# Attention weights times values in one encoder layer on one Trainium2 core: one fp32 product, or three fp32r products with low parts made on VectorE

## What is computed

```
logits = einsum('bqhcd,bkhcd->bhcqk', q, k) * scale + bias        # c = 0, 1; 512 x 512
p      = softmax(logits)
attn   = p[:, :, 0] - lam * p[:, :, 1]
out    = einsum('bhqk,bkhe->bqhe', attn, v)                       # v: 512 keys x 128
out    = rmsnorm(out, subln_g) * (1 - lambda_init)
```

## Time and profile before

| | |
|---|---|
| median of 3 runs | 968.12 us (967.98 to 968.15) |
| the profiled execution | 968.37 us, of which the span of instructions is 966.5 us |
| PE busy | 959.1 us, 99% of the span |
| DVE busy | 690.2 us, 71% |
| ACT busy | 439.5 us, 45% |
| granted TensorE clock, mean | 0.999 of full speed |

### The profile page before, as it was taken

One profiled execution on the slowest core, in us unless ns is written; L12 is line 12 of the kernel. 1 busy time (PEld: TensorE's weight loads), 2 busy tenths in 40 slices (PEclk: granted clock), 3 DMA queues, 4 the chain that ended last, 5 costly groups with the idle time before them and its releaser, 6 DMA issues.

```text
span 966.5 us, 15092 instructions
## 1 busy us (share of the span) xinstructions
PE 959.1 (99%) x5483; PEld 826.3 (85%) x5483; DVE 690.2 (71%) x1067; ACT 439.5 (45%) x699; POOL 87.9 (9%) x104
## 2 busy tenths in 40 slices
PE   9999999999999999999999999999999999999998
PEld 8889999999888887677777878889999999988887
DVE  6888897787754438868898755789897788743333
ACT  6445665546333233234454563446565554622222
POOL 0011121210011010000000000001112121000100
PEclk9999999999999999999999999999999999999999
DMA  6356767675433336121221332256777767333322
GB/s 231 139 142 170 194 166 193 179 184 150 137 97 101 98 124 241 66 83 51 83 85 44 121 109 91 95 142 154 191 189 171 197 169 190 100 104 98 90 68 87
DMA packets 55029, 128.67 MB, mean 133 GB/s; under 512 B 5954, under 2 KB 14287, under 8 KB 54724
## 3 DMA queue, kind: packets, MB, share of 16 engines
q1 hardware_dynamic: 44452, 107.31, 34.4%
q0 software_dynamic: 10384, 20.67, 12.3%
q10 hardware_dynamic: 144, 0.05, 0.1%
HBM read 123.78 MB, written 4.22 MB: 132 GB/s over the span
## 4 chain that ended last, share of the span: by engine, by line
PE 91%; DVE 5%; issue 2%; ACT 2%; DMA 0%; DVEq 0%; SPq 0%; ACTq 0%
PE bank L2159 14%; PE bank L2161 14%; PE bank L2160 14%; PE bank L2215 8%; PE bank L2216 8%; PE bank L2217 8%; PE bank L2207 6%; PE bank L2209 3%; PE bank L2656 1%; PE bank L2657 1%; PE bank L2658 1%; PE bank L2548 1%; DVE xt_both L1383 1%; PE bank L2302 1%; PE bank L2303 1%
## 5 line engine op out<-in xcount | busy, mean ns | idle before, releaser
L1220 DVE TENSOR_TENSOR w_lo<-raw,w_hi 128x1024 fp32r<-128x1024 f32 (+1 forms) x94 | 113.2, 1205 | 110.2 <-ACT w_hi L634 109.9
L634 ACT CAST w_hi<-raw 128x1024 fp32r<-128x1024 f32 (+1 forms) x94 | 95.0, 1011 | 187.5 <-PE bank L2161 172.5
L2159 PE MATMUL bank<-x_hi,w_hi 128*128 128x512 f32 x320 | 128.5, 402 | 0.1
L2160 PE MATMUL bank<-h_lo,w_hi 128*128 128x512 f32 x330 | 128.4, 389 | 0.0
L2161 PE MATMUL bank<-x_hi,w_lo 128*128 128x512 f32 x320 | 124.8, 390 | 0.0
L2160 PE MATMUL bank<-x_lo,w_hi 128*128 128x512 f32 x320 | 124.6, 389 | 0.0
L2215 PE MATMUL bank<-xt_both,w_hi 128*128 128x256 f32 x408 | 115.6, 283 | 1.0 <-ACT chain L786 1.0
L2217 PE MATMUL bank<-xt_both,w_lo 128*128 128x256 f32 x408 | 115.5, 283 | 0.0
L2216 PE MATMUL bank<-xt_both,w_hi 128*128 128x256 f32 x408 | 115.5, 283 | 0.0
L2215 PEld LDWEIGHTS bank<-xt_both,w_hi 128*128 128x128 f32 x408 | 78.2, 192 | 1.4 <-issue 1.4
L2217 PEld LDWEIGHTS bank<-xt_both,w_lo 128*128 128x128 f32 x408 | 78.2, 192 | 0.0
(11 more groups left out here) (382 smaller groups left out, 2138.0 us busy)
## 6 DMA issues: line engine op xcount, KB each, us to landing
raw<-in_ffn_w_down SPq DMA_DIRECT2D x32, 512.0 KB, 3.6
raw<-in_ffn_w_gate SPq DMA_DIRECT2D x25, 512.0 KB, 3.9
raw<-in_ffn_w_up SPq DMA_DIRECT2D x25, 512.0 KB, 4.4
raw<-in_w_in SPq DMA_DIRECT2D x24, 512.0 KB, 3.3
raw<-in_ffn_w_gate SPq DMA_DIRECT2D x34, 256.0 KB, 3.1
raw<-in_ffn_w_up SPq DMA_DIRECT2D x34, 256.0 KB, 3.1
raw<-in_ffn_w_down SPq DMA_DIRECT2D x16, 384.0 KB, 3.1
sums<-in_ffn_w_gate SPq DMA_DIRECT2D x17, 256.0 KB, 3.6
```

The source lines that it names most:

```text
L634: nc.scalar.copy(w_hi[:, half, 0:kb, :], raw[:, slot, 0:kb, :]).then_inc(w_hi_made, 1)
L1220: nc.vector.tensor_tensor(w_lo[:, half, 0:kb, :], raw[:, slot, 0:kb, :], w_hi[:, half, 0:kb, :].bitcast(F32), ALU.subtract).then_inc(w_spl ...
L2159: nc.tensor.matmul(dst, w_hi[:, half, k, :], hi, start=first and k == 0, stop=False)
L2160: nc.tensor.matmul(dst, w_hi[:, half, k, :], lo, start=False, stop=False)
```

## The change

It does five things.

1. The product of weights and values becomes three fp32r matmuls: v_hi by attn_hi, v_lo by attn_hi, v_hi by attn_lo. ACT's copies become casts to fp32r, as many as before. DVE gets five subtractions more for each head: `v_low(h)` and `attn_low(h, 0 to 3)`, 20 in all, each 128 x 512, reading a bank and the high part.
2. PE waits for these: the third matmul of a key block for its low part, a turn for the low part that frees its bank.
3. `attend_turns` moves ahead in the k-tile: behind group 5 of tile 13, behind group 4 of tiles 17 and 21. ACT takes the turned blocks ahead of the casts of q and k, and the cast of the next but one weight tile (15, 19, 23) behind them.
4. On DVE the low parts stand ahead of spectral pairs and of w_lo for tiles 14, 18 and 22, and some pairs move behind them, past the head's end.
5. Two small things far from there: the load of the lambdas counts on another semaphore, and one wait of DVE on itself uses a common counter.

```diff
-        v_nat, _ = place("v_nat", [P, NT, P], at=act3_at)
+        v_hi, _ = place("v_hi", [P, NT, P], F32R, at=act3_at)
+        v_lows = [place(f"v_lo{n}", [P, NT, P], F32R, at=at)[0] for n, at in enumerate((vx_at + 4 * S, bias_at))]
+        attn_hi, _ = place("attn_hi", [P, NT, S], F32R, at=attn_t_at)
```

ACT, the end of head 1 (heads 0 and 2 are alike):

```diff
             split(8, N_MIX + 18)
+            attn_turns(1, (0, 1))
             qk_high(2, 0)
-            attn_turns(1, (0, 1))
-            split(8, N_MIX + 19)
             qk_high(2, 1)
             attn_turns(1, (2, 3))
+            split(8, N_MIX + 19)
             attended(1)
```

DVE, the new functions:

```diff
+            def v_low(h):
+                dve.wait_ge(v_set, h + 1)
+                nc.vector.tensor_tensor(v_low_part(h)[:], bank[TURN_BANKS[h]][:].rearrange("p (t c) -> p t c", t=NT),
+                                        v_hi[:].bitcast(F32), ALU.subtract).then_inc(v_split, 1)
+
+            def attn_low(h, kt):
+
+                dve.wait_ge(attn_turned, NT * h + kt + 1)
+                dve.wait_ge(attn_t_set, NT * h + kt + 1)
+                nc.vector.tensor_tensor(attn_low_part(h, kt)[:], bank[4 + kt % 2][:], attn_hi[:, kt, :].bitcast(F32),
+                                        ALU.subtract).then_inc(attn_split, 1)
```

DVE, the end of head 0:

```diff
             combine(0, 3)
-            cross_far(0)
-            split(8, N_MIX + 14)
+            v_low(0)
+            attn_low(0, 0)
+            attn_low(0, 1)
             project(13)
             split_qk(1, 0)
+            attn_low(0, 2)
             split_qk(1, 1)
+            attn_low(0, 3)
+            split(8, N_MIX + 14)
+            cross_far(0)
             own_near(0)
             split(8, N_MIX + 15)
```

DVE, the end of head 1 and the begin of head 2 (at the end of head 2 `real_parities(1)` and `imaginary_parities(1)` move behind the low parts and w_lo of tile 22 in the same way):

```diff
             att_means(0)
-            imaginary_parities(0)
+            v_low(1)
             project(16)
-            split(8, N_MIX + 18)
-            cross_near(1)
+            attn_low(1, 0)
+            attn_low(1, 1)
             project(17)
             split_qk(2, 0)
+            attn_low(1, 2)
             split_qk(2, 1)
+            attn_low(1, 3)
+            split(8, N_MIX + 18)
+            imaginary_parities(0)
+            cross_near(1)
+            split(8, N_MIX + 19)
+
+            logits(2, 0)
             cross_far(1)
-            split(8, N_MIX + 19)
-
-            logits(2, 0)
-            own_near(1)
             combine(2, 0)
             logits(2, 1)
-            own_far(1)
+            own_near(1)
             project(18)
             combine(2, 1)
+            own_far(1)
             imaginary(1)
```

PE (`turn`, `attend`, and tile 17 for three tiles), and the two small things of point 5:

```diff
             def turn(h, kt):
-                wait(pe, attn_t_set, NT * h + kt - 1)
+                wait(pe, attn_split, NT * h + kt - 1)
...
                 for kt in range(NT):
                     pe.wait_ge(attn_t_set, NT * h + kt + 1)
-                    ins = nc.tensor.matmul(bank[6][:], v_nat[:, kt, :], attn_t[:, kt, :], start=kt == 0, stop=kt == NT - 1)
+                    nc.tensor.matmul(bank[6][:], v_hi[:, kt, :], attn_hi[:, kt, :], start=kt == 0, stop=False)
+                    nc.tensor.matmul(bank[6][:], v_low_part(h)[:, kt, :], attn_hi[:, kt, :], start=False, stop=False)
+                    pe.wait_ge(attn_split, NT * h + kt + 1)
+                    ins = nc.tensor.matmul(bank[6][:], v_hi[:, kt, :], attn_low_part(h, kt)[:], start=False, stop=kt == NT - 1)
...
-            project(17, between={6: lambda: attend_turns(1)})
+            project(17, between={4: lambda: attend_turns(1)})
...
-                dve.wait_ge(lam_landed, 16)
+                dve.wait_ge(mlp_landed, 32)
...
-                    nc.vector.tensor_tensor(hsum[:, 0, :], total, decay[:, 0, :], ALU.mult).then_inc(filt_read, 1)
-                    dve.wait_ge(filt_read, 1)
+                    link(nc.vector.tensor_tensor(hsum[:, 0, :], total, decay[:, 0, :], ALU.mult))
```

More of the change, by code:

```diff
@@ L222, in build, with v_low_part, attn_low_part @@
         assert top[0] <= tail_end
-        v_nat, _ = place("v_nat", [P, NT, P], at=act3_at)
+        v_hi, _ = place("v_hi", [P, NT, P], F32R, at=act3_at)
+        v_lows = [place(f"v_lo{n}", [P, NT, P], F32R, at=at)[0] for n, at in enumerate((vx_at + 4 * S, bias_at))]
+        attn_hi, _ = place("attn_hi", [P, NT, S], F32R, at=attn_t_at)
+        attn_lows = [place(f"attn_lo{n}", [P, S], F32R, at=at)[0]
+                     for n, at in enumerate((vx_at + 4 * 2 * S, vx_at + 4 * 3 * S, x0c_at + 4 * 3 * S))]
+        def v_low_part(h):
+            return v_lows[h == 3]
+        def attn_low_part(h, kt):
+            return attn_lows[1 if kt % 2 else 2 * (h == 3)]
         q_lo, _ = place("q_lo", [P, S], F32R, at=q_t_at)
@@ L281, in build @@
         x_landed = [sem(f"x_landed{k}") for k in range(KD)]
-        ident_landed, cols_landed, mlp_landed, lam_landed, dft_landed, late_landed, filt_landed = (
-            sem(n) for n in ("ident_landed", "cols_landed", "mlp_landed", "lam_landed",
+        ident_landed, cols_landed, mlp_landed, dft_landed, late_landed, filt_landed = (
+            sem(n) for n in ("ident_landed", "cols_landed", "mlp_landed",
                              "dft_landed", "late_landed", "filt_landed"))
@@ L427, in others @@
                 sp.dma_start(z_t[:], a["c_z"]).then_inc(mlp_landed, 16)
[L428 removed]
+                sp.dma_start(lam_in[:].rearrange("p k d -> p (k d)"), a["lambdas"].to_broadcast([P, 4 * DK])).then_inc(mlp_landed, 16)
                 sp.dma_start(rel[:], a["rel_bias"]).then_inc(late_landed, 16)
@@ L992, in v_natural @@
                 act.wait_ge(v_turned, h + 1)
-                nc.scalar.copy(v_nat[:], bank[TURN_BANKS[h]][:].rearrange("p (t c) -> p t c", t=NT)).then_inc(v_set, 1)
+                nc.scalar.copy(v_hi[:], bank[TURN_BANKS[h]][:].rearrange("p (t c) -> p t c", t=NT)).then_inc(v_set, 1)
             def attn_turns(h, kts):
@@ L998, in attn_turns @@
                     act.wait_ge(attn_turned, NT * h + kt + 1)
-                    nc.scalar.copy(attn_t[:, kt, :], bank[4 + kt % 2][:]).then_inc(attn_t_set, 1)
+                    nc.scalar.copy(attn_hi[:, kt, :], bank[4 + kt % 2][:]).then_inc(attn_t_set, 1)
             def attended(h):
@@ L2039, in _ @@
             att_means(1)
-            real_parities(1)
+            v_low(2)
             project(20)
-            split(8, N_MIX + 22)
-            imaginary_parities(1)
+            attn_low(2, 0)
+            attn_low(2, 1)
             project(21)
             split_qk(3, 0)
+            attn_low(2, 2)
             split_qk(3, 1)
+            attn_low(2, 3)
+            split(8, N_MIX + 22)
+            real_parities(1)
+            imaginary_parities(1)
             split(8, N_MIX + 23)
@@ L2079, in _ @@
             hy_low(3)
+            v_low(3)
+            attn_low(3, 0)
+            attn_low(3, 1)
             split(8, N_OUT + 1)
+            attn_low(3, 2)
+            attn_low(3, 3)
             split(8, N_OUT + 2)
@@ L2448, in two_scores @@
                     pe.wait_ge(logit_set, 2 * NT * h)
-                    pe.wait_ge(attn_t_set, NT * h)
+                    wait(pe, attn_split, NT * h)
                 for q in (qb, qb + 1):
@@ L2502, in turn_v @@
                 pe.wait_ge(spec_read, 2)
-                wait(pe, v_set, h)
+                wait(pe, v_split, h)
                 if h == 3:
@@ L2718, in _ @@
             project(12)
-            project(13, between={6: lambda: attend_turns(0)})
+            project(13, between={5: lambda: attend_turns(0)})
             attend(0)
@@ L2738, in _ @@
             project(20)
-            project(21, between={6: lambda: attend_turns(2)})
+            project(21, between={4: lambda: attend_turns(2)})
             attend(2)
```

24 lines of the change are left out of this document (12 added, 12 removed).

## The result

The changed kernel takes 972.68 us (median of 4 runs, 972.46 to 972.83), the kernel before 968.10 beside it (4 runs, 967.98 to 968.15): ratio 1.0049, 95% interval 1.0037 to 1.006, so 4.6 us slower. Its profiled execution is one of 972.83 us with a span of 970.9.

The account below looks back on a forecast made before the run. PE, busy 99% of the span, bounds the kernel, with DVE nearly full in the mixing stage. DVE's lateness makes the read-out 4.5 us late, less 0.35 from head 3's attend: 968.12 + 4.15 = 972.3 us; 8 in 10 range 969.0 to 975.5.

Parts of the forecast that it names:

- gain of `attend`: PE's attend stage in each head, shortened by three fp32r products but held by late low parts: 0.25 to 0.5 us.
- logits of head 1, 2, 3 on DVE: Start of DVE's logits at each head's end, put 3.2, 3.65 and 5.4 us late by the subtractions.
- turns of heads 1 and 2 held: PE's turns in tiles 17 and 21, moved earlier, wait for attn from DVE: 0.45 us in each head.
- w_lo(20), w_lo(21) hold PE: Head 2's weight tiles: DVE finishes their low parts late and PE waits, 0.95 and 0.85 us.
- PE waits ahead of inverse(0), starts: First inverse, behind head 3's logits on DVE: PE waits 2.1 us and is 4.1 us late.
- 1.6 us** are left of 3.6: Attend stages of all four heads: late low parts on DVE cut PE's gain from 3.6 to 1.6 us.
- the sign that the prediction named: Attend of head 0: about 4.25 us if the forecast is right, near 3.7 if wrong.
- 3.6 us in all: Attend stages of four heads: PE's gain if nothing is late, each attend then lasting 3.74 us.
- Rival 1: DVE keeps up, PE waits only inside attend: 966.5 us, or 964.5 with low parts in time; chance 0.10.
- rival 2: Weights late on DVE but 2 us made up before head 3's logits, inverse in time: 969.7 us; chance 0.14.
- rival 4: Worse: slower subtractions or waits not overlapping gains, 973.8 to 975.5 us, or PE's clock falls, 977.7; chance 0.12.
- 3.0 us of gain on paper: PE's products: three fp32r at 0.68 us, 0.19 less than one fp32, times 16 key blocks.

Follow-up runs that it names:

- 970.56: Changed kernel with head 3's DVE order altered: logits(3, 0) ahead of the second parity step, logits(3, 1) ahead of w_lo(23); 970.56 us, ratio 1.0029.
- the runs with GpSimd: All 32 spectral operations moved from DVE to GpSimd, in the changed kernel (976.94 us) and in the kernel before (974.93 us).
- the last run: Changed kernel, DVE order altered: k_lo earlier, head 3's logits earlier, cross_far(0) and a head 1 parity step in idle time, w_lo(20) ahead of a spectral step; 968.11 us.

## Why the prediction was right

Forecast 972.3 (4.15 slower), measured 972.68 (4.6 slower; the span 4.4). Its steps:

| step | forecast | trace of the changed kernel |
|---|---|---|
| fp32r product, start to start | 0.23, behind turns 0.31 | 0.23 and 0.32 |
| gain of `attend`, heads 0, 1, 2, 3 | 0.25, 0.5, 0.5, 0.35 | -0.06, 0.28, 0.24, 0.15 |
| four turns ahead of a product | 0.43 | 0.35 (462.77 to 463.12) |
| subtraction, start to start | 0.6 | 0.60 |
| logits of head 1, 2, 3 on DVE | 471.0, 503.8, 537.9 | 471.00, 503.74, 537.79 |
| w_lo(17) holds PE | 0.45 | 0.15 (488.03, and 487.88 by the distances of 0.23) |
| turns of heads 1 and 2 held | 0.45 each | 0.35 each (rows: 0.19 and 0.18) |
| w_lo(20), w_lo(21) hold PE | 0.95, 0.85 | 0.61, 0.85 (rows: 0.47 and 0.69) |
| w_lo(17), (20), (21) done on DVE | 488.12, 515.8, 522.2 | 487.89, 515.53, 521.95 |
| scores of head 3 on PE | 533.3 | 533.44 |
| PE waits ahead of inverse(0), starts | 2.1, 542.6 | 1.99 (row: 1.83), 542.60 |
| first read-out on DVE | 545.4 | 545.39 |

PE's waits stand in the table from start to start: how much later an instruction starts than it would by the distances that the trace has without a wait. The rows count idle time only behind the modelled end of the matmul ahead.

DVE's side stands: its logits and the read-out agree within 0.15 us, the three w_lo were done 0.23 to 0.27 earlier than forecast. Here a list of instructions on a nearly full engine could be added up. Shown by experiment are: that the subtractions make the loss (5.1 us), and that the wait at the inverse is for the logits of head 3 that stand behind other work (2.1 us).

The term that was mis-sized is the gain of `attend`, "**1.6 us** are left of 3.6". It measured 0.6 us in all (head 3 by the start of the second matmul behind it). From the end of the last attn_lo PE needs 0.48 us to the start of the scores (466.15 to 466.63) and not 0.25, and in head 0 it had begun 0.13 earlier. Of the sign that the prediction named, `attend` of head 0 at about 4.25 us, the trace has 4.55; and PE's share, which was to fall below 99%, still rounds to it (959.3 of 970.9 us).

Up to the scores of head 3 this is 0.8 us less gain than forecast (0.46 instead of 1.25). The waits of PE at w_lo and at the turns up to there were forecast too long by as much, 2.3 instead of 3.15 us in all, since PE came later and three w_lo were earlier. The two errors cancel, and behind them PE goes by DVE's times, as the first inverse waits for DVE's logits; this is why the sum came out, and is no proof of its terms. What does not cancel is head 3's own `attend`: the read-out is 4.51 us late, and with 0.15 us given back behind it instead of 0.35 this makes the 4.4 by which the spans differ.

The "3.6 us in all" that three products would give with no low part late is not seen either: with no low parts at all they gave 1.45 us, and 1.4 against one fp32 product beside the same subtractions. For the first the trace shows most of the reason. `attend` gave 1.6 us there, and of the 2.0 that are missing, 1.3 are the waits for ACT's copy in heads 1 and 2; the sum had taken all four heads down to 3.74 us.

The moved order of spectral work had no price of its own in the sum. It costs some 0.8 us where nothing needs it, and gains 1.3 us by most spans, 2.7 by the medians, where the low parts are there. I had it as places in a list, and did not see that DVE would stand idle in front of what was moved ahead. That idle time is 1.65 us in head 0 and 1.12 in heads 1 and 2. Filling a part of it in all heads (with w_lo(20) ahead of a spectral step) gave 2.45 us back, between the runs of 970.56 and 968.11, and the logits of head 3 ahead of work with time to spare gave the other 2.1.

Rival 1 (DVE keeps up) and rival 2 (weights late, inverse in time) fell with these rows; the run with head 3's logits first, in which the inverse is in time, comes within 0.9 us of rival 2's time. Of rival 4 the clock did not fall in the changed kernel, where the longest wait is 1.83 us; it did in the runs with GpSimd, behind 5.3 and 5.9 us. The sentence of the Trainium skill that the prediction weighed (page "TensorE: Matmul & The Clock Gate", section "HAM oscillation — how this bites in real kernels") agrees with these two runs, where the clock stood at 0.50 behind the waits, and had no price in the change itself.

## What to carry to other kernels

Work moved from a full engine to one that is nearly full costs what that engine's slack says at the next place where it is waited for, not on average: 3.0 us of gain on paper stood against 12 us of subtractions on an engine busy for 71% of the span, but for about 90% from 440 to 506 us. When small urgent operations are put ahead in a hand-written list, look for brackets of idle time on the late engine itself, put work without a deadline into them, and take what another engine waits for ahead of it: here that alone was worth as much as the whole loss (972.68 to 968.11 us).

## What the hardware showed unexpectedly

- With GpSimd's 128 x 512 operations beside it (1.3 to 2.3 us each where the trace has them singly), DVE's joining of two maps, with two SBUF operands, went from 0.75 to between 1.67 and 1.86 us, and instructions that read a bank stayed at 0.68.
- A product that had to wait for its low part was followed by the next product after 0.34 us instead of 0.23 (465.01 to 465.35 in head 0), and by the scores after 0.42 instead of 0.33 (in the last run, without the wait). About 0.1 us is lost behind such a wait, beside the wait itself.
- Behind a wait of 5.26 us the clock was granted at 0.50 of full speed up to 468.0 us and at 1.00 from 468.8 on, which cost the eight turns alone 0.9 us; behind one of 5.93 us it was 0.50 up to 471.0. Behind 1.83 us it stayed at 1.00.
